# A hybrid streaming encoder step: the sample attention unrolled, its probability transposes and values product moved between the next stream's score chunks

## The reference, cut to what matters

```
s = einsum('bqhd,bkhd->bhqk', q, K) * HEAD_DIM ** -0.5 + Fq[..., None] - Fk      # 16 x 1040 per head
s = where(k_pos <= q_pos, s, -inf)
p = softmax(s, axis=-1)
o = einsum('bhqk,bkhd->bqhd', p, V)                                              # 16 x 64 per head
b = o * silu(gate)
```

## Time and profile before

| | |
|---|---|
| median of 3 runs | 1659.38 us (1656.78 to 1661.76) |
| the profiled execution's own time | 1661.34 us |
| its span | 1659.5 us |
| PE busy | 1549.9 us, 93% of the span |
| DVE, ACT, POOL busy | 830.2, 632.3 and 400.0 us |
| sample attention | from 1247.8 to 1442.1 us of the span |

### The profile page before, as it was taken

How to read it: one execution, slowest core, us unless ns; L and a number is a source line. 1 busy time by engine, 2 the same in 40 slices (tenths; PEclk the granted TensorE clock), 3 DMA queues, 4 the chain that set the end, 5 groups by cost and what they waited for, 6 DMA issues and landing times. The chain is left out here.

```text
span 1659.5 us, 25036 instructions
## 1 busy us (share of the span) xinstructions
PE 1549.9 (93%) x9264; PEld 1365.9 (82%) x9264; DVE 830.2 (50%) x2094; ACT 632.3 (38%) x1347; POOL 400.0 (24%) x681
## 2 busy tenths in 40 slices
PE   6999999999999999996999999999996999689999
PEld 6997888778899898994888888888884777568887
DVE  3333022332444313125888898898884777442221
ACT  4443121110212001004978888787772344131010
POOL 1110015555200000002444344344313453100000
PEclk9999999999999899996999999999997999889999
DMA  5423122121201101005123223223106664263441
GB/s 150 147 102 97 46 78 80 63 77 45 81 24 36 42 23 34 15 14 115 47 68 74 61 54 74 60 58 70 31 11 228 213 205 158 99 221 124 143 152 64
DMA packets 181556, 144.60 MB, mean 87 GB/s; under 512 B 104063, under 2 KB 140832, under 8 KB 181440
## 3 DMA queue, kind: packets, MB, share of 16 engines
q1 hardware_dynamic: 178928, 134.08, 27.5%
q10 hardware_dynamic: 2448, 8.91, 1.3%
q0 software_dynamic: 64, 0.07, 0.1%
HBM read 106.50 MB, written 36.53 MB: 86 GB/s over the span
## 5 line engine op out<-in xcount | busy, mean ns | idle before, releaser
L920 PE MATMUL in_ps<-in_w_hi,in_xt_hi 128*128 128x512 f32 (+1 forms) x680 | 242.5, 357 | 4.9 <-DVE in_w_lo L648 3.4
L920 PE MATMUL in_ps<-in_w_hi,in_xt_lo 128*128 128x512 f32 (+1 forms) x680 | 239.7, 353 | 0.0
L920 PE MATMUL in_ps<-in_w_lo,in_xt_hi 128*128 128x512 f32 (+1 forms) x680 | 239.1, 352 | 0.0
L1421 DVE CUSTOM_DVE_ANT_0 pa_s_ring<-pa_ps_s,pa_f_b 128x512 f32<-128x512 f32 (+2 forms) x320 | 193.4, 604 | 43.6 <-PE pa_ps_s L1557 39.1
L927 PE MATMUL in_ps<-in_xt_hi,in_w_hi 128*128 128x384 f32 (+1 forms) x576 | 196.7, 341 | 8.2 <-DVE in_w_lo L648 8.2
L1500 DVE TENSOR_TENSOR pa_pt_lo<-pa_ps_t,pa_pt_hi 128x512 fp32r<-128x512 f32 (+2 forms) x320 | 193.1, 606 | 21.2 <-ACT pa_pt_hi L1395 18.5
L927 PE MATMUL in_ps<-in_xt_hi,in_w_lo 128*128 128x384 f32 (+1 forms) x576 | 192.1, 334 | 0.0
L927 PE MATMUL in_ps<-in_xt_lo,in_w_hi 128*128 128x384 f32 (+1 forms) x576 | 191.8, 333 | 0.0
L1395 ACT ACTIVATE pa_pt_hi<-pa_ps_t 128x512 fp32r<-128x512 f32 (+2 forms) x320 | 166.6, 534 | 51.6 <-PE pa_ps_t L1566 50.5
L1566 PE MATMUL pa_ps_t<-ident,pa_s_ring 128*128 128x128 f32 x1088 | 174.8, 276 | 8.3 <-DVE pa_pt_lo L1500 5.1
L1582 PE MATMUL pa_ps_o<-pa_pt_hi,pa_vs 128*128 128x256 f32 x576 | 162.8, 300 | 0.4 <-DVE pa_parts L1449 0.3
(11 more groups left out here) (252 smaller groups left out, 2829.8 us busy)
## 6 DMA issues: line engine op xcount, KB each, us to landing
sa_k_c<-in_cache_k_dram SPq DMA_DIRECT2D x8, 2048.0 KB, 8.6
sa_v_c<-in_cache_v_dram SPq DMA_DIRECT2D x8, 2048.0 KB, 8.6
in_w_raw<-in_w_in_dram SPq DMA_DIRECT2D x48, 256.0 KB, 3.8
out_dram<-in_out SPq DMA_DIRECT2D x34, 256.0 KB, 2.0
out_dram<-op_y ACTq DMA_DIRECT2D x17, 512.0 KB, 5.1
in_x<-in_x_prompt_dram SPq DMA_DIRECT2D x16, 512.0 KB, 3.5
op_x<-in_x_prompt_dram SPq DMA_DIRECT2D x16, 512.0 KB, 4.9
pa_f_b<-scratch_f SPq DMA_DIRECT2D x29, 256.0 KB, 5.0
```

The source lines that it names most:

```text
L920: mm = pe.matmul(ps[:, u % NBANK, 0:n], xa[:, k, at], wa[:, k, c0:c0 + n], start=(k == 0 and q == 0), stop=(k == KT - 1 and q == 2))
L1421: done = dve.tensor_tensor_reduce(scores_of(j)[:, b * P:(b + nb) * P], ps_s[:, (h * NQD + at) % 3, 0:nb * P], f_b[:, h % 2, b * P:(b + nb) ...
```

## The change

Four things are edited, all in `sample_attention`. The loops over the streams are unrolled on all engines, and the `waited` increments go. `turn_p(b - 1)`, which stood behind `score(b, 2)`, is cut: its banks 0 and 1 now stand behind `score(b, 0)`, its ninth tile behind `score(b, 1)`. `values(b - 1)` stands behind that tile, in front of `score(b, 2)`. ACT's `high_p` and DVE's `low_p` are cut and moved in the same way; `low_v` and `output` keep their place at the end of DVE's stream.

```
@@ scalar
-            def body(b, par, before, after):
+            for b in range(NB):
                 high_k(b, 2)
-                if after:
+                if b:
+                    high_p(b - 1, (0, 1))
+                if b + 1 < NB:
                     high_k(b + 1, 0)
+                if b:
+                    high_p(b - 1, (2,))
+                if b + 1 < NB:
                     high_k(b + 1, 1)
-                if before:
-                    high_p(b - 1)
-                exps(b, par)
...
@@ vector
-            def body(b, par, before, after):
+            for b in range(NB):
+                par = b % 2
                 low_k(b, 2)
                 minima(b, par, 0)
-                if after:
+                if b:
+                    low_p(b - 1, (0, 1))
+                if b + 1 < NB:
                     low_k(b + 1, 0)
                 minima(b, par, 1)
-                if after:
+                if b:
+                    low_p(b - 1, (2,))
+                if b + 1 < NB:
                     low_k(b + 1, 1)
                 minima(b, par, 2)
                 dve.wait_ge(chunk_min, b * NC_ + NC_)
                 dve.tensor_reduce(low[:, par, 3:4], low[:, par, 0:3], AX_X, ALU.min).then_inc(row_min, 1)
-                if before:
-                    low_p(b - 1)
                 for quarter in range(4):
                     low_v(b, par, quarter)
-                if before:
+                if b:
                     output(b - 1, 1 - par)
...
@@ tensor
-            def turn_p(b, par):
-                pe.wait_ge(exp_done, b * NC_ + NC_)
-                for n, tiles in enumerate(PB):
+            def turn_p(b, par, part):
+                if part[0] == 0:
+                    pe.wait_ge(exp_done, b * NC_ + NC_)
+                for n in part:
+                    tiles = PB[n]
...
-            def body(b, par, before, after):
+            for b in range(NB):
+                par = b % 2
+                after = b + 1 < NB
                 score(b, par, 0, lambda n: turn_k(b, par, 2, n))
+                if b:
+                    turn_p(b - 1, 1 - par, (0, 1))
                 score(b, par, 1, (lambda n: turn_k(b + 1, 1 - par, 0, n)) if after else (lambda n: None))
+                if b:
+                    turn_p(b - 1, 1 - par, (2,))
+                if b:
+                    values(b - 1, 1 - par)
                 score(b, par, 2, (lambda n: turn_k(b + 1, 1 - par, 1, n)) if after else (lambda n: None))
-                if before:
-                    turn_p(b - 1, 1 - par)
-                    values(b - 1, 1 - par)
-
-            streams(pe, body)
-            turn_p(NB - 1, 1)
+            turn_p(NB - 1, 1, (0, 1, 2))
             values(NB - 1, 1)
```

More of the change, by code:

```diff
@@ L1712, in sample_attention @@
         block = ctx.enter_context(nc.Block())
[L1714 to L1722, removed]
         def count(b, par, unit):
@@ L1833, in lay_q @@
                     cols = slice(NQ * half, NQ * half + NQ)
-                    src = q_t[rows, :, ds(b * NQ, NQ)]
+                    src = q_t[rows, :, b * NQ:(b + 1) * NQ]
                     hi = qz_hi[rows, par, :].rearrange("p (a c) -> p a c", c=160)[:, :, cols]
@@ L1860, in _ @@
             lay_q(0, 0)
-            def body(b, par, before, after):
-                if after:
-                    lay_q(b + 1, 1 - par)
-                split_v_hi(b, par)
-            streams(pool, body)
+            for b in range(NB):
+                if b + 1 < NB:
+                    lay_q(b + 1, 1 - b % 2)
+                split_v_hi(b, b % 2)
         def k_banks(b, c):
@@ L1896, in _ @@
             high_k(0, 1)
-            def body(b, par, before, after):
+            for b in range(NB):
                 high_k(b, 2)
-                if after:
+                if b:
+                    high_p(b - 1, (0, 1))
+                if b + 1 < NB:
                     high_k(b + 1, 0)
+                if b:
+                    high_p(b - 1, (2,))
+                if b + 1 < NB:
                     high_k(b + 1, 1)
-                if before:
-                    high_p(b - 1)
-                exps(b, par)
-            streams(act, body)
-            high_p(NB - 1)
+                exps(b, b % 2)
+            high_p(NB - 1, (0, 1, 2))
         @block.vector
@@ L1937, in low_v, with low_p @@
                                   ALU.subtract).then_inc(vl_done, 1)
-            def low_p(b):
-                for n, tiles in enumerate(PB):
+            def low_p(b, part):
+                for n in part:
+                    tiles = PB[n]
                     dve.wait_ge(p_h, b * 3 + n + 1)
@@ L1995, in body @@
                     dve.wait_ge(gates_in, 16 * (NB - 2))
-            streams(dve, body)
-            low_p(NB - 1)
+            low_p(NB - 1, (0, 1, 2))
             output(NB - 1, 1)
@@ L2268, in encoder_layer @@
         ident = whole.enter_context(nc.sbuf_tensor("ident", [P, P], F32))
-        waited = whole.enter_context(nc.semaphore("waited"))
         input_stage(nc, ident, x_prompt, x_sample, norm_g, w_in, q_norm_g, k_norm_g, b_f, cache_logf,
```

33 lines of the change are left out of this document (12 added, 21 removed).

## The result

The changed kernel takes **1702.93 us** (median of 4 runs, 1699.42 to 1706.58) beside 1660.57 us for the kernel before (4 runs): a ratio of 1.0252, with a 95% interval of 1.0235 to 1.0268. The profiled execution took 1706.58 us with a span of 1704.9 us, 45.4 us more than before.

The account below looks back on a forecast made before the run. PE, busy 93% of the span, was taken as the bound. -11.1 + 16.2 + 22.2 + 4.2 + 8.4 + 2 = +41.9 us gave 1703.2, or 1701 against the median; range over the cases 1680 to 1724, forecast's chance 0.71.

Parts of the forecast that it names:

- The removed stall: PE's wait of the ninth probability tile's transpose for `low_p` goes in iterations 1 to 7: -11.1 us.
- Wait one: At six stream boundaries, PE's first matmul waits for the exponential of chunk 0: 2.7 us each, +16.2.
- T: The moment at a stream boundary at which PE could go on to the next stream.
- Wait two: Third key transpose of chunk 0 waits for `low_k` behind `low_v` and `output`: 3.7 us at six boundaries, +22.2.
- the prediction's sign was 2 to 4: Sign of being right: the third key transpose of streams 2 to 7 waits 2 to 4 us for `low_k`.
- The clock: Half clock behind each of six boundaries until T + 12.2: 1.4 us each, +8.4; bounds 0 and 4.9.
- The rival of long spells: Clock stays low for 9.8 us behind wait two, 4.9 instead of 1.4 per boundary: 1722 us, chance 0.16.
- the prediction's sign was 26 to 28: Sign of being right: a stream takes 26 to 28 us instead of 21.2.
- the end and its clock: After the last stream's scores, `low_v`, `output`, ninth tile and products stand bare: +4.2; half clock in `values(7)`: +2.
- The unrolling: Loops written out and increments dropped in the sample attention: cost put at 0.
- V's load: SP's load and POOL's split of the next V: ready at T + 20, 7 us to spare, cost 0.
- `low_p` between `minima` and `low_k`: DVE's `low_p` of banks 0 and 1 before the next stream's first `low_k`: put at 0, uncovered up to 0.5 per stream.

Follow-up runs that it names:

- the run with the cut `turn_p` and the values last: Changed kernel with only the values product put back behind the third score chunk: 1655.56 us, ratio 0.998, where 1649 us was expected.
- with wait one filled: Changed kernel plus 14 unread matmuls on PE behind the third score chunk of streams 1 to 6: 1701.64 us, ratio 1.0251.
- The run with both waits filled: Changed kernel plus 14 unread matmuls behind the third score chunk and 20 before the third key transpose of chunk 0: 1690.17 us, ratio 1.0184.
- the version with V in halves and the fill: Kernel with values behind the third score chunk and V loaded in two halves, plus 14 unread matmuls between streams 0 and 1: 1650.95 us, ratio 0.9943.

## Why the prediction was right, point by point

- **The removed stall, -11.1.** Right. No ninth tile of streams 0 to 6 waits, and the run with the cut `turn_p` and the values last shows that this part does no harm. That it brings so little alone was foreseen neither here nor in that run's expectation; in the changed kernel, where streams are longer, V is never late.
- **Wait one, 2.7 per boundary.** Right to a tenth: 2.50 or 2.51 us idle and T + 2.7 at every boundary.
- **Wait two, `low_k` at T + 9.4.** Right in its place: T + 9.3. The idle time shown, 1.2 to 3.5 us where the prediction's sign was 2 to 4, is below the 3.7 of the sum, because a PE at half clock fills a part of it with the same work; at full clock, with wait one filled, it is 3.5. The run with both waits filled gives the two terms clean: 25.74 us per stream, against 21.2 - 1.7 + 2.7 + 3.7 = 25.9 forecast.
- **The clock, 1.4 per boundary.** The mechanism is right and the size too small: 2.4 us. The sum took the spell of the earlier trace rows, which ended at T + 12.2. In the boundary shown it begins later behind the wait (at 1334.1, T + 4.3), lasts 10.1 us and ends at T + 14.4, which leaves 5.0 us behind wait two at half clock instead of 2.8, and half of 5.0 is about the 2.4. At the other five boundaries the spells end between T + 13.6 and T + 16.9, all later than T + 12.2. One spell of the kernel before was taken for all; in the changed kernel they last 7 to 14 us. This is the step that was mis-sized, by 1.0 us per boundary. The rival of long spells had 4.9 per boundary; the measured 2.4 is between, nearer to the forecast. Streams came out at 27.5 to 29.0 us, where the prediction's sign was 26 to 28.
- **Between the starts of streams 1 and 7.** The terms of the sum that lie there are six stalls, six times wait one, and five times wait two and clock: -10.0 + 16.2 + 18.5 + 7.0 = +31.7. Measured: (1444.60 - 1279.06) - (1410.96 - 1279.87) = +34.5. The 2.8 between are a difference of larger errors: the clock took 5 us more than the sum has, the two waits took 1 us less, and stream 1, by itself, 1.4 less. It took 24.8 us after 25.1 before, where the sum has +1.0, which fits its half clock: it ended at 1286.4 and not, as before, at 1289.7. Why the spell was shorter is not shown.
- **From the start of stream 7 to the end.** Here lie the last stall, one wait two, one clock term, the end and its clock: -1.1 + 3.7 + 1.4 + 4.2 + 2 = +10.2. Measured: (1487.05 - 1444.60) - 31.14 = +11.3, right to 1 us, about what the clock was mis-sized by. In this stretch all of `values(7)` up to 1480.90 ran at half clock.
- **What was put at 0.** The unrolling: 0.999, no change by its interval. V's load: POOL's split for stream 3 starts at 1345.71 and `low_v` needs it at 1359.50; never waited for. PE's waits show none that `low_p` between `minima` and `low_k` would have caused.
- **Why the whole agrees to 2 us.** The two stretches give 45.8 us, and stream 1 starts 0.8 earlier: 45.0 in the profile, where the sum had 41.9. The profiled execution was also 3.6 us above its median, so the comparison of medians (+42.4) falls closer than the parts do. The mechanisms are shown; that the medians agree within 2 us is in part luck, since the clock was forecast 6 us too small over six boundaries and other differences took half of that back.

The page "TensorE: Matmul & The Clock Gate" of the Trainium skill (section "Why this matters for your kernels") warns of idle gaps between bursts of matmuls; this case's trace agrees, with a spell of half clock at each of the seven boundaries, 2.4 us per stream.

## What to carry to other kernels

Work that looks movable on the busiest engine may be the cover for a chain on others. Before moving it, write down which chain runs beside it (here minimum, reduction, exponential, 2.7 us; and `low_v`, `output`, `low_k`, 9.4 us), and keep the cover beside that chain, even where its own inputs are ready earlier. After a stall is removed, follow the buffers that are now needed sooner: here a load of V in two halves, the first issued earlier, turned a gain of 0.2% into 0.55%. And a gap filled with other work brought next to nothing here as long as a second gap followed it.

## What the runs showed of the hardware that was not expected

**DVE and POOL slow each other, and either can pay.** The four `low_v` quarters, each with two inputs in SBUF, take 4.62 us alone and 5.3 to 6.2 us beside several of POOL's small operations on V and queries (values last, streams 1 to 7); POOL's subtraction of 16x512 (L1834) takes 1.28 us ahead of `low_v` and 2.25 us beside it. POOL can also pay all of it: in the kernel before, a cast of 64x64 that takes 0.23 us alone starts at 1320.04, just ahead of `low_v` at 1320.14, and takes 4.81 us, while `low_v` takes its usual 4.6. The kernel that is merely unrolled shows the same (4.63 us for that cast in stream 2). The page "GPSIMD Engine Reference" of the Trainium skill (section "1. Specifications") says that GpSimd's access to SBUF is shared with VectorE, with contention when a DVE instruction has two SBUF inputs, and these traces agree. One consequence is that a stream that gets shorter can slow its own DVE chain.

**The length of the wait alone does not tell whether the clock falls.** Waits of 2.35 to 3.5 us, one or two in each stream with busy stretches between, brought the mean clock to 0.80 to 0.91 over five streams, and the six gaps of 1.0 to 1.5 us in the kernel before left it at 1.00. But there is no clean line between them. These are PE's rows for stream 7 of the kernel before, stream 2 of the version with V in halves and the fill, and stream 2 of the version with the values last:

```profile
1431.51 0.28 PE L2048 MATMUL sa_ps_p<-ident,sa_p 128*16 128x128 f32 x1 [1.83 <-DVE sa_p_lo L1945]
```

```profile
1304.34 0.60 PE L2002 MATMUL sa_ps_k<-ident,sa_k_c 128*128 128x128 f32 x3 [1.24 <-DVE sa_kt_lo L1913]
```

```profile
1305.10 0.60 PE L1997 MATMUL sa_ps_k<-ident,sa_k_c 128*128 128x128 f32 x3 [2.23 <-DVE sa_kt_lo L1908]
```

Behind the 1.83 us the clock was 0.50 from 1433.5 to 1436.3, and behind the 1.24 us it was 0.50 from 1306.3 to 1309.7; behind the 2.23 us it stayed at 1.00. So a gap left by an edit should be looked up in the trace and not judged by its length. What else decides was not tried.
